# Gate weights loaded in the scan, five gate products in its last read-out, and the first output panel ahead of the residual stream

## The chip, the cores and the metric

The kernel runs on one core of a Trainium2 chip. One launch computes a two-part transformer block stack from its inputs. The metric is the device time of the launch in microseconds (us); lower is better.

## The reference, cut to what matters

The program runs two layers of a first block (attention mixed with an mLSTM, then an RWKV mixer, each followed by an MLP) and then a second block (gated linear attention, pooling, experts). The change touches the RWKV mixer's read-out and output of layer 1, on 512 tokens with 1024 channels (16 heads of 64):

```python
g = jax.nn.sigmoid(xg @ g1) @ g2          # g1: 1024 x 160, g2: 160 x 1024
...
def readout(p, y_f, y_b):
    y = y_f + y_b                         # the two scan directions
    mean = jnp.mean(y, axis=-1, keepdims=True)
    var = jnp.mean(jnp.square(y - mean), axis=-1, keepdims=True)
    y = ((y - mean) * lax.rsqrt(var + RW_GN_EPS)).reshape(r.shape) * lnx_w + lnx_b
    coef = ...                            # sum of r * k_dir * r_k over directions and head
    bonus = (coef * split_heads(v, RW_HEADS, RW_HEAD_DIM)).reshape(r.shape)
    return ((y + bonus) * g).astype(h_l.dtype) @ w_o
x = x + gt_a * out_l                      # then the MLP of the layer
```

## The kernel before, in words

Activations lie transposed: channels on the 128 partitions, tokens along the columns, so 1024 channels are eight blocks m = 0 to 7. A `Kernel` object K hands each engine its own in-order list of instructions; producers count up one semaphore per engine, and consumers wait for a count. `fence(name)` (line 54) makes an engine wait until every engine has reached the same place; TensorE's own count is part of it. PSUM has eight banks of 128 by 512, handed out in turn by `K.bank` (line 169), which waits until the bank's last reader is done.

Large products are written as three fp32r products (high by high, high by low, low by high) by the class `Split` (line 700): ScalarE copies half a weight panel to a rounded version (`act`, line 717, with the instruction on line 720), VectorE subtracts it from the original (`dve`, line 722, instruction on line 725), and TensorE then runs the products (line 750). Small products, the gate's among them, are plain fp32, and each of these stands in the trace as two MATMUL records.

The scan is `rw_pe`, `rw_act`, `rw_dve` and `rw_pool`, all driven by one list of steps, `rw_turns` (line 2421). There are 24 units (8 blocks m by 3 token ranges) for each of two directions d, and twelve turns per unit. In each turn stand the steps `solve` of unit n, `prep` of unit n + 1, `stream` of unit n - 1, and the steps `end` of the block before: six steps of the read-out of block m (0: the sum of the directions on VectorE; 1: the mean's product on TensorE, line 2584, and the centring on VectorE, line 2742; 2: ScalarE's square, line 2867; 3: the variance's product, line 2588, VectorE, line 2746, and logarithm and exponential on ScalarE; 4: the product for `coef`, line 2592, scaling on VectorE, copy on ScalarE; 5: two VectorE operations, the last on line 2758). For blocks 0 to 6 these steps lie beside the scan of the next block. For block 7 nothing else is left on any engine.

Then comes the fence "rwkv". Behind it the output stage runs:
- SyncE (`rw_out_sp`, line 2941) issues, in this order, the load of the residual stream from its spill in DRAM into `K.Xf` (2 MB), the two panels of `w_o` (2 MB each), and the MLP's first panel (2 MB). Later panels wait for a free slot.
- GpSimd (`rw_out_pool`, line 2947) loads `g2` in two pieces, 128 rows (512 KB) and 32 rows (128 KB).
- TensorE (`rw_out_pe`, line 2953) waits for both, then forms the eight gate blocks, each as a product over 128 rows (line 2958) and one over 32 rows (line 2959), and then the products with `w_o` in four groups g of two output blocks.
- VectorE (`rw_out_dve`, line 2981) does `w.dve(0)`, then for each block m multiplies the read-out by the gate (line 2988) and, one block behind, subtracts the rounded version (line 2992), then `w.dve(1)`, then per output block the residual addition (line 3001).
- ScalarE (`rw_out_act`, line 2966) does `w.act(0)` and `w.act(1)`, rounds the eight gated blocks (line 2972), and then goes on to the other panel halves and the squares for the next norm.

In the scan GpSimd (`rw_pool`, line 2879) first loads nine constants and four lora tiles; per unit it then multiplies gains (lines 2906, 2908), `kr` (2915), the operands `bb`, `ks` (2920, 2922) and `rr` (2925), and in `stream` scales the state (2933). `K.load` is on line 183, panels on line 192.

Of the kernel before, what the change touches and what calls it, by code (L numbers as in the profile page):

```python
# [542 lines left out]
def plan_layer1(K, w_at):  # L543
    a = K.a1 = Box()
    a.vec, a.wa0, a.gh = K.Cf[:, 1984:2024], K.alloc(32), K.alloc(2, 512)
    K.align()
    a.mix_lo, a.mixf = K.rounded(K.top, 8, 772), K.flat(8 * 772)
    a.mix = a.mixf.rearrange("p (k t) -> p k t", k=8)
    a.kT = a.mixf[:, 0:6144].rearrange("p (k t) -> p k t", k=8)
    r_at = K.top  # L550
    a.r_lo, a.rT = K.rounded(K.top, 8, 768), K.alloc(8, 768)
    hp_at, hpf = K.top, K.flat(8 * 772)
    mark = K.top - 32
    a.hp = hpf.rearrange("p (k t) -> p k t", k=8)
    a.vT = hpf[:, 0:6144].rearrange("p (k t) -> p k t", k=8)
    a.hi = K.rounded(K.top, 8, 768)
    K.alloc(8, 768)
    a.xx_lo, a.xx = K.rounded(K.top, 8, 772), K.alloc(8, 772)
    K.top = r_at
    a.w1, a.a1, a.g1 = K.alloc(8, 128), K.alloc(8, 128), K.alloc(8, 160)  # L560
    a.mu, a.wh, a.ah = K.Cf[:, 0:48], K.Cf[:, 64:832], K.Cf[:, 832:1600]
    K.top = hp_at
    a.g2 = K.alloc(2, 1024)
    K.align()
    a.rhi, a.wo = K.rounded(K.top, 8, 512), K.rounded(K.top + 4096, 4096)
    K.alloc(8192)
    K.top = mark
    r = K.rw = Box()
    bk1 = K.alloc(512)
    keep = K.top  # L570
    K.top = w_at
    r.cn = {n: K.const(n) for n in ("m16_0", "m16_1", "m32_0", "m32_1", "m64_0", "m64_1", "i64", "si_0", "si_1")}
    r.kk = [K.alloc(768) for _ in range(2)]
    bk = [K.row, bk1]
    r.dirs = []
    ybufs = []
    for d in range(2):
        s = Box()
        s.NP, s.M, s.Pf = K.alloc(2, 4, 64), K.alloc(4, 64), K.alloc(4, 64)
        far = K.Xf[:, 2048 * d:2048 * d + 1280]  # L580
        s.sets = [(K.alloc(2, 4, 64), K.alloc(4, 2, 64), K.alloc(4, 64), K.alloc(2, 4, 64)),
                  (far[:, 0:512].rearrange("p (x g c) -> p x g c", x=2, g=4),
                   far[:, 512:1024].rearrange("p (g x c) -> p g x c", g=4, x=2),
                   far[:, 1024:1280].rearrange("p (g c) -> p g c", g=4),
                   bk[d].rearrange("p (a g c) -> p a g c", a=2, g=4))]
        s.RH, s.UU = K.alloc(64), [K.alloc(64) for _ in range(2)]
        s.zm, s.zg = [K.alloc(64) for _ in range(2)], K.alloc(64)
        s.tmp = [K.alloc(256) for _ in range(5)]
        s.ops = [K.alloc(4, 256) for _ in range(3)]
        s.me = [K.alloc(3, 2) for _ in range(3)]  # L590
        s.gn = [K.alloc(2) for _ in range(3)]
        s.wm = [K.alloc(2, 128) for _ in range(2)]
        r.dirs.append(s)
        ybufs += [K.alloc(512) for _ in range(2)]
        if d == 0:
            K.top = keep
    r.sq, r.kavh = K.alloc(768), K.Cf[:, 2024:2032]
    r.V = [K.Xf[:, o:o + 768].rearrange("p (x c) -> p x c", c=64) for o in (1280, 3328)]
    r.y = K.ring("y", ybufs)
    r.kr = K.several("kr", 4, 512)  # L600


def plan_block2(K):
# [1765 lines left out]
UNITS, TURNS = 24, 12  # L2369
# [51 lines left out]
def rw_turns(K):  # L2421

    for n in range(-2, UNITS + 2):
        for turn in range(TURNS):
            if (n + 2) % 3 == 0 and (n + 2) // 3 < 8 and turn <= 5:
                yield "kk", turn, (n + 2) // 3
            for d in range(2):
                if 0 <= n < UNITS:
                    yield "solve", turn, Unit(K, d, n)
                if 0 <= n + 1 < UNITS and turn in PREP:  # L2430
                    yield "prep", PREP[turn], Unit(K, d, n + 1)
            for d in range(2):
                if 1 <= n <= UNITS:
                    yield "stream", turn, Unit(K, d, n - 1)
            m, since = divmod(n, 3)
            if since < 2 and 1 <= m and turn + TURNS * since in END:
                yield "end", END[turn + TURNS * since], m - 1


def halves():  # L2440
    for hd in range(2):
        yield hd, slice(64 * hd, 64 * hd + 64)


def rw_pe(K):
    a, pe = K.a1, K.pe
# [24 lines left out]
    for what, turn, u in rw_turns(K):  # L2471
# [65 lines left out]
        if what == "stream":  # L2537
# [22 lines left out]
            if part == 2:  # L2560
                pe.wait_ge(K.at("uu in", *c), K.at("BK", *u.key))
                done = [("streamed", *c)] + ([("streamed", *u.key)] if sub == 3 else [])
                if u.next(sub):
                    ps = K.bank("zz", *c)
                    for k, w in enumerate((uu, vm)):
                        for hd, o in halves():
                            mm = pe.e.matmul(ps[o, 0:64], u.BK[o, k, g, :], w[o, :], start=k == 0, stop=k == 1,  # L2567
                                             skip_group_check=True)
                    mm.then_inc(*pe.up(("zz", *c), *([] if u.lat else done)))
                if u.lat:  # L2570
                    ps = K.bank("y", *c)
                    pe.wait_ge(K.at("Arb", *u.key))
                    sums = (zm, u.rr[:, cs]), (uu, u.Arb[:, g, :]), (vm, u.A[:, g, 1, :])
                    for k, (w, A) in enumerate(sums):
                        for hd, o in halves():
                            mm = pe.e.matmul(ps[o, 0:64], w[o, :], A[o, :], start=k == 0, stop=k == 2, skip_group_check=True)  # L2576
                    mm.then_inc(*pe.up(("y", *c), *done))
        if what == "end":
            m, y0, k0 = u, K.rw.y.of(0, u), K.rw.kr.of(0, u)
            y1 = K.rw.y.of(1, u)  # L2580
# [298 lines left out]
def rw_pool(K):  # L2879
# [10 lines left out]
        K.load(pool, K.rw.cn[n], K.const_src(n), "rw const", n)  # L2890
    for d in range(2):
        weights(d, 0)
    for what, turn, u in rw_turns(K):
        if what == "prep":
            s = u.s
# [2 lines left out]
            if turn == 3:  # L2898
                if u.b == 2 and u.m < 7:
                    weights(u.d, u.m + 1)  # L2900
                pool.wait_ge(K.at("me exp", *u.key))
                if u.n >= 3:
                    pool.wait_ge(K.at("streamed", u.d, u.n - 3))
                if u.b:
                    last = Unit(K, u.d, u.n - 1)
                    pool.e.tensor_tensor(u.gn[:, 0:1], last.me[:, 2, last.xl[1]:last.xl[1] + 1],
                                         u.me[:, 0, u.xl[0]:u.xl[0] + 1], MUL).then_inc(*pool.up())
                pool.e.tensor_tensor(u.gn[:, 1:2], u.me[:, 2, u.xl[0]:u.xl[0] + 1], u.me[:, 0, u.xl[1]:u.xl[1] + 1],
                                     MUL).then_inc(*pool.up(("gain", *u.key)))
            if turn == 4 and u.lat:  # L2910
                if u.b == 1:
                    s.kb, free_k = K.rw.kr.take(u.d, u.m)
# [26 lines left out]


def rw_out_sp(K):
    K.load(K.sp, K.Xf, K.spill, "rw back")
    for i in range(2):
        K.panel_in(K.D["w_o"][i], "rw out", i)


def rw_out_pool(K):
    D, a, pool = K.D, K.a1, K.pool
    K.load(pool, a.g2[:, 0, :], D["g2"][0:128, :], "g2")
    K.load(pool, a.g2[0:32, 1, :], D["g2"][128:160, :], "g2 rest")  # L2950


def rw_out_pe(K):
    a, pe = K.a1, K.pe
    pe.wait_ge(K.at("g2"), K.at("g2 rest"))
    for m in range(8):
        ps = K.bank("rw gate", m)
        pe.e.matmul(ps, a.g2[:, 0, m * 128:m * 128 + 128], a.gh[:, 0, :], start=True, stop=False)
        pe.e.matmul(ps, a.g2[0:32, 1, m * 128:m * 128 + 128], a.gh[0:32, 1, :], start=False, stop=True).then_inc(
            *pe.up(("rw gate", m)))  # L2960
    for g in range(4):
        through(rw_out(K).columns(g, "rw out", 2 * g, lambda k, x0, x1: (a.rhi[:, k, x0:x1], a.r_lo[:, k, x0:x1]), LAT,
                                  lambda k: K.at("rw out lo", k), wide=g == 0))
# [1 line left out]

def rw_out_act(K):
    a, s, w, mlp = K.a1, K.act, rw_out(K), Mlp(K, 1)
    for g in range(2):
        w.act(g)
    for k in range(8):  # L2970
        s.wait_ge(K.at("rw gated", k))
        s.e.activation(a.rhi[:, k, :], a.rT[:, k, 0:512], ACT.Copy).then_inc(*s.up(("rw out hi", k)))
    for m in range(8):
        if m in (0, 2):
            w.act(2 + m // 2)
# [4 lines left out]

def rw_out_dve(K):
    a, v, w, mlp, LP = K.a1, K.dve, rw_out(K), Mlp(K, 1), K.mod[1][:, 0, :]
    w.dve(0)
    for m in range(9):
        if m < 8:
            r = a.rT[:, m, 0:512]
# [2 lines left out]
        if m:  # L2989
            r = a.rT[:, m - 1, 0:512]  # L2990
            v.wait_ge(K.at("rw out hi", m - 1))
            v.e.tensor_tensor(a.r_lo[:, m - 1, 0:512], r, a.rhi[:, m - 1, :], SUB).then_inc(*v.up(("rw out lo", m - 1)))
    w.dve(1)
    v.wait_ge(K.at("rw back"))
    for m in range(8):
# [1093 lines left out]
def pool_program(K):  # L4089
# [14 lines left out]
    pool.wait_ge(K.at("rw spill"))  # L4104
    rw_pool(K)
    pool.fence("rwkv")
    rw_out_pool(K)
    Mlp(K, 1).sums.pool()
    pool.fence("rw out")
    sums2(K).pool()  # L4110
# [74 lines left out]
```

## Time and profile before

| what | value |
|---|---|
| median of 3 runs | 3717.08 us (3716.05 to 3722.02) |
| the profiled execution's own time | 3724.84 us |
| its span, first to last instruction | 3723.0 us |
| TensorE matmul busy | 3426.0 us, 92% |
| VectorE, ScalarE, GpSimd busy | 44%, 32%, 11% |
| mean granted TensorE clock | 0.956 |

The span is cut by stage in the program's order: layer 0 first, the RWKV scan from about 1515 to 2290 us, its output stage from 2302 to 2395 us, then the MLP, the second block and the experts. A granted clock of 1.00 is 2.4 GHz and 0.50 is 1.2 GHz. Times in views are microseconds from the start of the span.

### The profile page before, as it was taken

The page shows a single profiled execution, that of the slowest core. Times are in us where ns is not written, and L with a number is a line of the kernel's source. Part 1 is how long each engine was busy: PE and PEld are TensorE (multiplying, and loading weights), DVE is VectorE, ACT ScalarE, POOL GpSimd, SP SyncE. Part 2 cuts the span into 40 slices and gives each one's busy share as a digit, 9 for nine tenths or more (in the row PEclk, how much of TensorE's full clock was granted, in tenths as well). Part 3 has the DMA queues.
Part 4 walks back from the last instruction along what each step waited for, and adds up shares of the span by engine and source line. Part 5 has one row for each costly group of instructions (what it writes and reads, how often), then busy time and mean ns, then how long its engine had stood idle before and what let it go on. Part 6 is the DMA issues. An engine that isn't in the chain of part 4 may idle for free.

```text
span 3723.0 us, 79537 instructions
## 1 busy us (share of the span) xinstructions
PE 3426.0 (92%) x35550; PEld 2659.8 (71%) x35550; DVE 1632.2 (44%) x3121; ACT 1179.5 (32%) x2462; POOL 394.4 (11%) x616
## 2 busy tenths in 40 slices
PE   7898998999999799799999997999999899799998
PEld 5767877788888388688888895588878677433332
DVE  3354455433333732466666663443443474312112
ACT  3342233312212332355555543222233332200001
POOL 0000122000000100232222221000010300000000
PEclk8999999999999899899999997899999899799999
DMA  4493162211111110000000002122211122689996
GB/s 177 149 352 111 51 241 108 79 58 68 68 61 54 65 46 23 10 5 5 5 5 4 5 5 99 46 91 102 102 66 46 47 104 76 264 353 412 414 428 293
DMA packets 35237, 437.42 MB, mean 117 GB/s; under 512 B 5024, under 2 KB 5632, under 8 KB 9168
## 3 DMA queue, kind: packets, MB, share of 16 engines
q1 hardware_dynamic: 29664, 413.44, 27.8%
q0 software_dynamic: 5232, 18.89, 1.6%
q8 instruction: 280, 4.59, 0.5%
q14 instruction: 61, 0.50, 0.0%
HBM read 425.49 MB, written 6.82 MB: 116 GB/s over the span
## 4 chain that ended last, share of the span: by engine, by line
PE 80%; DMA 7%; DVE 6%; ACT 5%; issue 1%; POOL 0%; SPq 0%; DVEq 0%; ACTq 0%; POOLq 0%
PE ps L750 23%; PE ps L2045 8%; PE ps L2047 8%; PE ps L2046 8%; PE ps L2461 7%; PE ps L3816 6%; DMA part<-in_wu 4%; PE ps L2454 3%; PE ps L1005 2%; PE ps L2468 2%; PE ps L2576 1%; ACT L71 1%; PE ps L2567 1%; DMA part<-in_wd 1%; PE ps L1322 1%
## 5 line engine op out<-in xcount | busy, mean ns | idle before, releaser
L750 PE MATMUL ps<-part 128*128 128x256 f32 (+1 forms) x4848 | 879.3, 343 | 40.9 <-DVE part L990 15.5
L750 PEld LDWEIGHTS ps<-part 128*128 128x128 f32 x4848 | 756.5, 193 | 160.6 <-issue 19.1
L2045 PE MATMUL ps<-part 128*128 128x512 f32 (+1 forms) x1536 | 549.6, 358 | 18.0 <-DVE part L2092 11.4
L2046 PE MATMUL ps<-part 128*128 128x512 f32 (+1 forms) x1536 | 548.8, 357 | 0.0
L2047 PE MATMUL ps<-part 128*128 128x512 f32 (+1 forms) x1536 | 548.6, 357 | 0.0
L3816 PE MATMUL ps<-part 128*64 128x512 f32 x1536 | 374.8, 606 | 27.4 <-DMA part<-in_wg 12.2
L2069 DVE TENSOR_TENSOR part<-part 128x1024 fp32r<-128x1024 f32 x128 | 158.3, 1237 | 497.7 <-ACT part L2058 497.7
L2461 PE MATMUL ps<-part 64*64 64x64 f32 x9984 | 344.7, 220 | 20.5 <-ACT part L2784 11.9
L2461 PEld LDWEIGHTS ps<-part 64*64 64x64 f32 x9984 | 319.1, 136 | 51.2 <-ACT part L2784 12.9
L2045 PEld LDWEIGHTS ps<-part 128*128 128x128 f32 x1536 | 289.7, 189 | 68.5 <-DVE part L2092 12.6
L2046 PEld LDWEIGHTS ps<-part 128*128 128x128 f32 x1536 | 290.5, 189 | 46.9
L2047 PEld LDWEIGHTS ps<-part 128*128 128x128 f32 x1536 | 289.7, 189 | 47.1
L3816 PEld LDWEIGHTS ps<-part 128*64 128x64 f32 x1536 | 119.6, 139 | 262.9 <-issue 201.9
L2058 ACT ACTIVATE part<-part 128x1024 fp32r<-128x1024 f32 x128 | 135.5, 1059 | 489.9 <-PE ps L2047 489.9
L725 DVE TENSOR_TENSOR part<-part 128x2048 fp32r<-128x2048 f32 x54 | 123.5, 2292 | 264.8 <-ACT part L720 264.6
L840 POOL TENSOR_TENSOR part<-part 128x512 f32<-128x512 f32 (+1 forms) x42 | 49.2, 1181 | 1217.2 <-ACT part L832 1216.7
L720 ACT ACTIVATE part<-part 128x2048 fp32r<-128x2048 f32 x58 | 110.4, 1910 | 95.0 <-PE ps L750 71.4
L3893 DVE TENSOR_TENSOR part<-part,ps 128x512 f32<-128x512 f32 x32 | 22.0, 687 | 244.6 <-PE ps L3790 115.1
L2454 PE MATMUL ps<-part 64*64 64x64 f32 (+1 forms) x2816 | 110.1, 229 | 11.3 <-DVE part L2661 11.3
L2454 PEld LDWEIGHTS ps<-part 64*64 64x64 f32 x2816 | 101.6, 137 | 11.7 <-DVE part L2661 11.7
L2833 ACT ACTIVATE part<-ps 128x512 f32<-128x512 f32 x144 | 75.2, 529 | 92.3 <-PE ps L2461 92.3
L2468 PE MATMUL ps<-part 64*64 64x64 f32 x2688 | 95.9, 219 | 0.8 <-DVE part L2697 0.6
(418 smaller groups left out, 4362.9 us busy)
## 6 DMA issues: line engine op xcount, KB each, us to landing
part<-in_ada_w SPq DMA_DIRECT2D x36, 2048.0 KB, 9.7
part<-in_mlp_w SPq DMA_DIRECT2D x32, 2048.0 KB, 7.5
part<-in_wg SPq DMA_DIRECT2D x32, 2048.0 KB, 14.1
part<-in_wu SPq DMA_DIRECT2D x32, 2048.0 KB, 13.0
part<-in_wd SPq DMA_DIRECT2D x32, 2048.0 KB, 14.3
part<-in_b_in SPq DMA_DIRECT2D x8, 2048.0 KB, 7.7
part<-in_ab_w_in SPq DMA_DIRECT2D x7, 2048.0 KB, 8.3
part<-in_rkv SPq DMA_DIRECT2D x6, 2048.0 KB, 7.5
```

The lines of the kernel that those rows point to most:

```text
L720: s.e.activation(self.first(g), self.tile(g), ACT.Copy).then_inc(*s.up((name, "rounded", g), (name, "split", g)))
L725: v.e.tensor_tensor(self.rest(g), self.tile(g), self.first(g), SUB).then_inc(*v.up((name, "split", g)))
L750: mm = pe.e.matmul(ps[:, j * n:j * n + n], lhs, rhs, start=k == ks[0] and i == 0, stop=k == ks[-1] and i == 2)
L2045: pe.e.matmul(ps, wh[:, k, :], hi[:, k, x0:x1], start=k == 0, stop=False)
L2046: pe.e.matmul(ps, wh[:, k, :], lo[:, k, x0:x1], start=False, stop=False)
L2047: mm = pe.e.matmul(ps, wl[:, k, :], hi[:, k, x0:x1], start=False, stop=k == 7)
L2058: s.e.activation(b.W[t % 2][0], src, ACT.Copy).then_inc(*s.up(self.key("rounded", t), self.key("split", t), *([("free", "w") + self.key("w ...
L2069: v.e.tensor_tensor(wl, src, wh, SUB).then_inc(*v.up(self.key("split", t), *([("free", "w") + self.key("w", p)] if c == 3 else [])))
L2454: mm = pe.e.matmul(out[o, 2 * it + j], lhs[o, t], rhs[o, :, t], start=True, stop=True)
L2461: mm = pe.e.matmul(ps[h, o + g * 64:o + g * 64 + 64], lhs[h, g, :], rhs[h, g, :], start=True, stop=True)
L2468: mm = pe.e.matmul(ps[h, o + i * 64:o + i * 64 + 64], block[h, :], K.ident[h, h], start=True, stop=True)
L3816: mm = pe.e.matmul(ps[half(p), :], lhs(k, p), K.panel(8, 512, w, g, c, p)[:, k, :], start=k == 0, stop=k == 7)
```

## The change

The second piece of `g2` gets two places of its own that are free during the scan (`rest`, and one at the end), and the first piece takes the place in `K.Cf` where the lora inputs of the scan lay. GpSimd issues the two loads of the second piece at the head of the scan, and the load of the first in the preparation of the last unit, once the last lora products have read that place. Gate blocks 0, 1 and 2 to 4 are issued by TensorE within the read-out of block 7, after its steps 0, 2 and 4; blocks 5 to 7 stay behind the fence. SyncE loads the first panel of `w_o` ahead of the residual stream and the second panel behind it. ScalarE rounds gated blocks 0 to 5, then does `w.act(0)`, then blocks 6 and 7, then `w.act(1)`; VectorE does `w.dve(0)` after all the gated blocks. The arithmetic is unchanged.

```diff
@@ plan_layer1
     K.top = hp_at
-    a.g2 = K.alloc(2, 1024)
+    K.alloc(2048)
...
         if d == 0:
+            rest = K.alloc(512)
             K.top = keep
...
+    a.g2, a.g2r = K.Cf[:, 64:1088], [rest, K.alloc(512)]
@@ rw_turns
             if since < 2 and 1 <= m and turn + TURNS * since in END:
                 yield "end", END[turn + TURNS * since], m - 1
+                if m == 8 and END[turn + TURNS * since] in (0, 2, 4):
+                    yield "gate", END[turn + TURNS * since], None
...
+def gate_pe(K, m):
+
+    a, pe = K.a1, K.pe
+    ps = K.bank("rw gate", m)
+    c = slice(m % 4 * 128, m % 4 * 128 + 128)
+    pe.wait_ge(K.at("g2"), K.at("g2 rest", m // 4))
+    pe.e.matmul(ps, a.g2[:, m * 128:m * 128 + 128], a.gh[:, 0, :], start=True, stop=False)
+    pe.e.matmul(ps, a.g2r[m // 4][0:32, c], a.gh[0:32, 1, :], start=False, stop=True).then_inc(*pe.up(("rw gate", m)))
@@ rw_pe
+        if what == "gate":
+            for m in {0: (0,), 2: (1,), 4: (2, 3, 4)}[turn]:
+                gate_pe(K, m)
         if what == "end":
@@ rw_pool
     for d in range(2):
         weights(d, 0)
+    for i in range(2):
+        K.load(pool, a.g2r[i][0:32, :], D["g2"][128:160, i * 512:i * 512 + 512], "g2 rest", i)
...
+            if turn == 4 and u.n == UNITS - 1 and u.d:
+                pool.wait_ge(*[K.at("lora", d, UNITS - 1) for d in range(2)])
+                K.load(pool, a.g2, D["g2"][0:128, :], "g2")
             if turn == 4 and u.lat:
@@ rw_out_sp
-    K.load(K.sp, K.Xf, K.spill, "rw back")
     for i in range(2):
         K.panel_in(K.D["w_o"][i], "rw out", i)
-
-
-def rw_out_pool(K):
-    D, a, pool = K.D, K.a1, K.pool
-    K.load(pool, a.g2[:, 0, :], D["g2"][0:128, :], "g2")
-    K.load(pool, a.g2[0:32, 1, :], D["g2"][128:160, :], "g2 rest")
+        if i == 0:
+            K.load(K.sp, K.Xf, K.spill, "rw back")
@@ rw_out_pe
-    pe.wait_ge(K.at("g2"), K.at("g2 rest"))
-    for m in range(8):
-        ps = K.bank("rw gate", m)
-        pe.e.matmul(ps, a.g2[:, 0, m * 128:m * 128 + 128], a.gh[:, 0, :], start=True, stop=False)
-        pe.e.matmul(ps, a.g2[0:32, 1, m * 128:m * 128 + 128], a.gh[0:32, 1, :], start=False, stop=True).then_inc(
-            *pe.up(("rw gate", m)))
+    for m in range(5, 8):
+        gate_pe(K, m)
@@ rw_out_act
-    for g in range(2):
-        w.act(g)
     for k in range(8):
         s.wait_ge(K.at("rw gated", k))
         s.e.activation(a.rhi[:, k, :], a.rT[:, k, 0:512], ACT.Copy).then_inc(*s.up(("rw out hi", k)))
+        if k == 5:
+            w.act(0)
+    w.act(1)
@@ rw_out_dve
-    w.dve(0)
     for m in range(9):
...
+    w.dve(0)
     w.dve(1)
     v.wait_ge(K.at("rw back"))
@@ pool_program
-    rw_out_pool(K)
```

## Rows read from the trace of the kernel before

**Rows 1.** The page: shares of the chain that ended last.

```profile
PE 80%; DMA 7%; DVE 6%; ACT 5%; issue 1%; POOL 0%; SPq 0%; DVEq 0%; ACTq 0%; POOLq 0%
```

**Rows 2.** The chain of waits, 2288 to 2395 us: start, length, who held it.

```profile
2288.73 0.94 PE ps L2576 x24
...
2290.76 1.14 PE ps L2584 x2
2291.92 0.70 DVE part L2742
2292.65 0.64 ACT part L2867
2293.33 2.09 PE ps L2588 x2
...
2300.98 0.70 DVE part L2758
...
2302.90 13.42 DMA part<-in_g
2316.45 2.04 PE ps L2958 x2
...
2348.54 46.29 PE ps L750 x192
```

**Rows 3.** Windows: length, busy time of the five engines, granted clock, DMA share, GB/s.

```profile
2284.00:2290.00 6.00, 5.35 (x144) 4.55 (x140) 1.13 (x4) 3.14 (x14) 0.59 (x2) 1.00 0.02 5
2290.00:2293.00 3.00, 1.12 (x2) 0.30 (x2) 2.47 (x4) 0.35 (x1) 0.00 (x0) 0.92 0.00 0
2293.00:2295.00 2.00, 1.67 (x2) 0.84 (x3) 0.00 (x0) 0.28 (x1) 0.00 (x0) 0.50 0.00 0
...
2328.40:2336.40 8.00, 8.00 (x9) 2.00 (x8) 2.58 (x4) 1.26 (x2) 0.00 (x0) 0.50 0.00 0
...
2352.00:2360.00 8.00, 8.00 (x33) 6.50 (x32) 0.85 (x1) 0.00 (x0) 0.00 (x0) 0.88 0.00 0
```

**Rows 4.** Timeline and window of the lora products of line 2299, about 1290 us.

```profile
1283.86 14.29 PE L2299 MATMUL ps<-part 128*128 128x512 f32 x28
...
1282.80:1298.00 15.20, 15.20 (x31) 3.18 (x30) 15.13 (x19) 4.88 (x11) 0.00 (x0) 1.00 0.00 1
```

**Rows 5.** Timeline of GpSimd, and its DMAs of line 183 from 1480 us on.

```profile
1528.93 0.35 POOL L2908 TENSOR_TENSOR part<-part 128x1 f32<-128x1 f32 x1 [13.51 <-ACT part L2805]
...
2234.17 0.73 POOL L2915 TENSOR_TENSOR part<-part 128x256 f32<-128x256 f32 x1 [2.26 <-DVE part L2654]
2235.26 0.73 POOL L2915 TENSOR_TENSOR part<-part 128x256 f32<-128x256 f32 x1 [0.36 <-DVE part L2654]
...
2240.19 1.59 POOL L2925 TENSOR_TENSOR part<-part 128x256 f32<-128x256 f32 x2 [0.96 <-ACT part L2811]
...
L183 POOL DMA_DIRECT2D part<-in_w x16: 524/536/577, 1513.3 to 2143.0; - x16
...
DMA to landing us min/median/max: 1.9/2.1/13.4
```

**Rows 6.** DMA issues of 2270 to 2420 us; then line 192's (five panels) landing.

```profile
part<-spill SPq DMA_DIRECT2D x1, 2048.0 KB, 8.5
...
DMA to landing us min/median/max: 7.4/14.7/23.5
```

**Rows 7.** Timeline of the output stage: single operations of VectorE and ScalarE.

```profile
2319.00 2.29 DVE L725 TENSOR_TENSOR part<-part 128x2048 fp32r<-128x2048 f32 x1 [17.33 <-ACT part L720]
...
2324.54 0.69 DVE L2988 TENSOR_TENSOR part<-part,ps 128x512 f32<-128x512 f32 x1 [2.65 <-PE ps L2959]
2325.14 0.68 DVE L2992 TENSOR_TENSOR part<-part 128x512 fp32r<-128x512 f32 x1
2325.26 0.63 ACT L2972 ACTIVATE part<-part 128x512 fp32r<-128x512 f32 x1 [2.70 <-DVE part L2988]
...
2362.27 1.92 ACT L720 ACTIVATE part<-part 128x2048 fp32r<-128x2048 f32 x1 [12.35 <-PE ps L750]
```

## The prediction

> **What bounds the kernel now.** I read the page first: TensorE is 92% busy and holds 80% of the chain that ended last [rows 1], so only what leaves that chain counts. The change touches one place, from the end of the recurrent scan to the first product with `w_o`, so the next view is the chain of waits over that stretch. It shows four pieces in a row [rows 2]. The last scan product ends at 2288.73 + 0.94 = 2289.67 us. The read-out of the last column block goes back and forth between the engines until VectorE's last addition ends at 2300.98 + 0.70 = 2301.68, which opens the fence. Then a DMA of the gate's weights holds everything until 2316.3. Then sixteen gate products, two for each of eight blocks, run to 2348.54, where the first product with `w_o` starts. From the fence to that product it is 2348.54 - 2301.68 = 46.9 us, of which 14.8 us are the wait and 32.1 us the gate.
>
> The third view is the windows of that stretch. One fp32 product of 512 columns takes 32.1 / 16 = 2.00 us here [rows 2], and the granted clock is 0.50 (1.2 GHz) in all of it, although TensorE is 100% busy [rows 3]. The clock was 1.00 (2.4 GHz) in the scan, 0.92 over 2290 to 2293, and 0.50 from 2293 on, after TensorE had worked 1.12 of 3 us. It came back only under the `w_o` products. At 1.00 the same kind of product costs half: before the r, k, v projections a run of alternating products, 128 by 128 and 128 by 32, of 512 columns kept 1.00 throughout and did 28 records (14 products) in 14.29 us, so 1.02 us each [rows 4]. One block of the gate is thus 4.01 us at half clock and 2.04 us at full.
>
> **Part 1: the weights are loaded in the scan.** This removes the wait of 14.6 us for the DMA. It adds three DMAs on GpSimd. The two of the 32 remaining rows stand at the head of the scan behind 13 others of the same kind; at about 0.53 us of issue each [rows 5] they end before GpSimd's first arithmetic there; I take 0, at worst 2 x 0.53 = 1.1 us. The large one stands in unit 23's preparation, d = 1. Its wait for the lora products is one that the engine's next input already implies. It costs 0.53 us of issue between the two `kr` products of 2234.17 and 2235.26. Between these GpSimd was idle 0.36 us, and the 0.2 us left over meets an idle 0.96 us ahead of `rr` [rows 5]. Behind the load wait the products that make unit 23's operands, and TensorE's gram behind these. I take 0, at most 0.5 us. It has from about 2235 to 2289.7 to land; 13.4 us was the slowest of GpSimd's DMAs, under 8 MB of other traffic [rows 6].
>
> **Part 2: five gate blocks in the last read-out.** TensorE takes its work in program order, so each product that is put ahead can delay the read-out. At full clock, from 2289.67:
> - gate 0 runs to 2291.7. The mean's product was ready at 2290.76 [rows 2], so it is 0.95 us late and ends at 2292.8 (two records, about 1.0 us).
> - gate 1 runs to 2294.8. VectorE's centring, 0.70, and ScalarE's square, 0.64, would have released the variance's product at 2294.3 [rows 2], so it starts 0.5 us late and ends at 2295.9; `coef` at 2296.9; gates 2, 3 and 4 (6.1 us) at 2303.0.
> - the rest of the read-out took 2301.68 - 2295.42 = 6.26 us from the end of the variance's product [rows 2]; now it ends at 2302.1.
>
> The fence counts TensorE's work too, so it opens at 2303.0, 1.3 us later than before. The five blocks and the three others with the read-out take exactly the eight PSUM banks; all were freed before.
>
> Whether these products hold the full clock is the disputed cost, since no row has a product of 32 rows at 1.00. Bounds: 2.04 us a block by [rows 4], 4.01 by [rows 2]. I take 2.04, because TensorE goes without a gap from the scan into them, and a run with every second product narrow kept its clock [rows 4]; the runs at 0.50 all began after idling. Against this stands that 32 us of such work did not bring the clock back [rows 3].
>
> The Trainium skill (TensorE: Matmul & The Clock Gate, section "Why this matters for your kernels") says that continuous matmul work takes the array to its full clock and that idle gaps between bursts take it back. The trace agrees with the second half and not with the first: the gate ran 32 us without a gap at 0.50. By the rule the five blocks run at full clock, as I take it, and the three behind the fence do so as well.
>
> **Part 3: behind the fence (F = 2303.0).** Gate 5 needs the bank that VectorE frees with its first product, at F + 0.8. At full clock gates 5, 6, 7 end at F + 2.8, 4.9, 6.9. VectorE multiplies (0.69), ScalarE rounds (0.63), VectorE subtracts (0.68) [rows 7]; overlapped, a block costs VectorE about 1.26 us, so block 5 is multiplied by F + 6.6 and rounded by F + 7.3. Now ScalarE does `w.act(0)` (1.92), which needs the first panel. Before, that panel was second in SyncE's queue and landed 14.7 us after its issue; the first in the queue, the residual stream, took 8.5 us, and a panel alone 7.4 [rows 6]. I take 8.1, so the rounding runs from F + 8.2 to F + 10.1. Then block 6 is rounded by 10.8 and subtracted by 11.5, block 7 by 12.1, and `w.dve(0)` (2.29) ends at 14.4. The first `w_o` product starts at F + 14.5 = 2317.5. Cover: gate 7's end (F + 6.9) has 1.5 us of slack before VectorE's turn for it at F + 8.4; at half clock it would end at F + 12.8. The start then is late by the chain behind the gate: 0.69 + 0.63 + 0.69 + 2.29, so at F + 17.2.
>
> **Part 4: panel order.** The residual stream now lands second, within 15 us, and is wanted first more than 10 us after the first `w_o` product. Panel 1 is third in the queue as before. Both cost 0. The second half's split is done before it is needed: 1.92 on ScalarE and 2.29 on VectorE lie beside about 11.6 us of the first products.
>
> **Sum.** 2348.54 - 2317.5 = 31.0 us less: 14.6 of wait, 32.1 of gate and 0.2 of issue leave; 1.3 comes before the fence and 14.5 behind it. The `w_o` products begin at half clock before and after, since TensorE idles ahead of them in both; I allow 1 us either way for when it rises. What follows is paced by TensorE, and SyncE's panels are released by its products, so it moves with it. The profiled execution takes 3724.84 - 31.0 = 3693.8 (span 3692), and it was 7.8 us above the median. The median: 3717.08 - 31.0 = 3686.
>
> **The rivals.**
> - A, the clock falls as before, after the mean's product. Gate 1 at half clock ends at 2296.8, variance 2298.8, `coef` 2300.8, three gates 2312.9. F is 2312.9, the start F + 17.2 = 2330.1: 18.4 us gained, 3698.7. For it: [rows 3], where the 32-row products never raised the clock, and the fall near 2292.5. Against it: the fall came after a stretch mostly idle, and now there is none. 14%.
> - B, the first panel comes no sooner than it did, after 14.7 us, because transfers queued behind it share the engines. ScalarE then splits from F + 14.9 to 16.8, and block 6, block 7 and the rest follow 6.7 us late: start F + 21.2 = 2324.2, 24.3 us gained, 3692.8. For it: 14.7 in [rows 6]. Against it: the queue's first took 8.5. 10%.
> - C, slower: the gate's large load lands late. Gate 0 then blocks TensorE's queue in front of the mean's product, and its price is the landing less 2289.7. The change turns slower at landings past 2320.7, 86 us after GpSimd's turn; one at 2330 costs 9 net: 3726. Against it: small loads land in 2.0 us and the longest took 13.4 [rows 5, 6]. 2%.
> - D, no change: the fence opens later by what leaves behind it, because the read-out is paced by the gate. It would take 31 us more ahead of the fence, and all five blocks at half clock are 20 us. 1%.
>
> **How the numbers follow.** My forecast has 73%, with its own range 3682 to 3691 (panel landing between 7.4 and 8.6, clock rise 1 us, issue costs to 1.6 us, drift between measurements 2 us). The range for 8 in 10 runs from 3681 to 3699 and takes in B and most of A. A measurement of this kernel can tell 0.2%, 7.4 us, from no change: every case but C and D is below 3709.6, so faster 0.97, same 0.01, slower 0.02.
>
> **What would show it.** Right: granted clock near 1.00 up to the fence, with gate records near 0.6 us; the mean's product starting at scan end + 2.0; no idle time for a load of `g2`; the fence 13.3 us after the scan's end (12.0 before); the first `w_o` product 14.5 us behind it, the last thing before it being VectorE's subtraction of the panel. Wrong: 0.50 within the read-out (A), ScalarE waiting beyond F + 9 for `w_o` (B), TensorE waiting for `g2` at the scan's end (C), or a scan longer by over 1 us.

## The result, and the profile after

| | before | after |
|---|---|---|
| median, first comparison | 3717.84 us (3716.05 to 3722.02, 4 runs) | 3690.47 us (3686.91 to 3693.23, 4 runs) |
| ratio, 95% interval | | 0.9919 (0.9907 to 0.9931) |
| median, repeat | 3719.7 us (9 runs) | 3690.4 us (3687.49 to 3695.69, 5 runs), ratio 0.9919 (0.9905 to 0.9933) |
| profiled execution: own time, span | 3724.84, 3723.0 us | 3686.91, 3685.1 us |
| scan's end to the first `w_o` product | 58.9 us | 26.8 us |
| scan's end to the MLP's first product | 113.1 us | 80.8 us |

The ratio makes the changed kernel 30.1 us faster (25.7 to 34.6); the medians differ by 27.4 and 29.3 us. The forecast was 31.0. The changed kernel is faster clear of the noise. The profiled execution of before was its slowest and that of after its fastest, so their spans differ by 37.9 us: 1.7 us of that lie ahead of the scan's end, where both run the same code but for the three loads of `g2`, 32.4 us in the stretch that was changed, and 3.8 us behind it.

The chain of waits of the changed kernel over the read-out and the output stage (start, length, who held it) answers to [rows 2]; lines 2456 and 2457 are the two products of a gate block:

```profile
2287.01 0.92 PE ps L2591 x24
2287.92 1.05 PE ps L2456 x2
2288.98 1.05 PE ps L2457 x2
2290.03 1.06 PE ps L2602 x2
...
2292.99 1.06 PE ps L2606 x2
...
2299.98 1.06 PE ps L2457 x2
2301.04 0.02 issue
2301.06 7.55 DMA part<-in_w_o
2308.61 0.02 issue
2308.64 1.91 ACT part L723
2310.55 0.53 ACT part L2984
2311.07 0.02 issue
2311.10 1.29 DVE part L3006 x2
2312.39 2.21 DVE part L728
2314.60 0.14 issue
2314.74 5.41 PE ps L753 x13
```

The chain is now TensorE without a gap from the scan's end, 2287.92, to the fence at 2301.04, then the first panel's landing, then the splits. The gate's load has gone from it. The windows show the clock; their columns are those of [rows 3]:

```profile
2291.00:2295.00 4.00, 4.00 (x10) 1.47 (x9) 1.38 (x2) 0.83 (x2) 0.00 (x0) 1.00 0.00 0
2295.00:2301.00 6.00, 6.00 (x12) 1.48 (x10) 2.62 (x4) 2.94 (x4) 0.00 (x0) 1.00 0.00 0
2301.00:2308.50 7.50, 6.39 (x13) 1.77 (x12) 7.25 (x12) 3.67 (x6) 0.00 (x0) 1.00 0.89 339
2308.50:2314.70 6.20, 0.00 (x0) 0.00 (x0) 4.93 (x7) 4.75 (x4) 0.00 (x0) 0.56 1.00 428
2314.70:2318.00 3.30, 3.26 (x8) 2.62 (x9) 2.10 (x1) 0.00 (x0) 0.00 (x0) 0.50 1.01 432
```

Where the read-out had 0.50 before, it has 1.00, and so have the three blocks behind the fence here. TensorE then idles 6.5 us and begins `w_o` at half clock, as before. On GpSimd the large load stands where it was expected, in the timeline that answers to [rows 5]:

```profile
2231.25 0.73 POOL L2938 TENSOR_TENSOR part<-part 128x256 f32<-128x256 f32 x1 [2.26 <-DVE part L2672]
2231.92 0.60 POOL L183 DMA_DIRECT2D part<-in_g  x1
2232.54 0.74 POOL L2938 TENSOR_TENSOR part<-part 128x256 f32<-128x256 f32 x1
```

### The profile page after: what moved, and what is told of

It is laid out like the page before. It is cut to its first block, busy times and chain, and to the rows that moved or that the text cites. A ratio compares the mean times of both kernels' runs of the same rounds, so it can differ in the third digit from the quotient of the medians.

```text
span 3685.1 us, 79537 instructions
## 1 busy us (share of the span) xinstructions
PE 3399.3 (92%) x35550; PEld 2654.1 (72%) x35550; DVE 1632.4 (44%) x3121; ACT 1178.6 (32%) x2462; POOL 394.9 (11%) x617
## 4 chain that ended last, share of the span: by engine, by line
PE 80%; DMA 7%; DVE 6%; ACT 5%; issue 1%; POOL 0%; SPq 0%; DVEq 0%; ACTq 0%; POOLq 0%
PE ps L753 23%; PE ps L2048 8%; PE ps L2050 8%; PE ps L2049 8%; PE ps L2476 7%; PE ps L3831 6%; DMA part<-in_wu 4%; PE ps L2469 3%; PE ps L2483 2%; PE ps L1008 1%; PE ps L2591 1%; ACT L71 1%; PE ps L2582 1%; PE ps L1325 1%; PE ps L3711 1%
## 5 line engine op out<-in xcount | busy, mean ns | idle before, releaser
L2469 PEld LDWEIGHTS ps<-part 64*64 64x64 f32 x2816 | 102.2, 137 | 12.1 <-DVE part L2679 12.1
```

The costliest lines, as they stand in the source:

```text
L2469: mm = pe.e.matmul(out[o, 2 * it + j], lhs[o, t], rhs[o, :, t], start=True, stop=True)
```

## The experiments

A place in the stage is given in us from the end of the last scan product: +16.3 is 16.3 us behind it. Each such figure is of one profiled execution. Edits are against the changed kernel.

### All eight gate blocks behind the fence

```diff
@@ rw_turns
-                if m == 8 and END[turn + TURNS * since] in (0, 2, 4):
-                    yield "gate", END[turn + TURNS * since], None
@@ rw_out_pe
-    for m in range(5, 8):
+    for m in range(8):
@@ gate_pe
-    pe.e.matmul(ps, a.g2r[m // 4][0:32, c], ...
+    pe.e.matmul(ps, a.g2r[1][0:32, c], ...
```

> The changed kernel with all eight gate blocks behind the fence and none in the read-out; the loads stay in the scan, the panel order and the order on ScalarE and VectorE stay (blocks 0 to 3 use the narrow weights of blocks 4 to 7, so the values differ, not the work). Measured from the end of the last scan product to the first w_o product, which is 58.9 us before and 26.8 us after. Theory: TensorE idles in the read-out, the granted clock falls to 0.50, and blocks with a 32-row product do not bring it back: fence at +12.0, eight blocks at 4.01 us, then 0.69 + 0.63 + 0.69 + 2.29, so 48.7 us; gain over before 10 us, near 3708. Rival: continuous matmul work brings the clock back in some 5 us as it did under the w_o products: block at 2.1 us after that, 36 us in all, near 3695.

Measured: 3712.54 us (10 runs), ratio 0.9977 (0.9968 to 0.9986); first `w_o` product 47.8 us from the scan's end. The windows:

```profile
2296.00:2300.00 4.00, 3.72 (x4) 1.00 (x4) 0.06 (x1) 0.00 (x0) 0.00 (x0) 0.50 0.74 233
2300.00:2312.00 12.00, 12.00 (x13) 3.00 (x12) 3.27 (x5) 1.89 (x3) 0.00 (x0) 0.50 1.01 431
2312.00:2328.40 16.40, 16.37 (x17) 4.00 (x16) 5.16 (x8) 4.32 (x5) 0.00 (x0) 0.50 0.32 139
```

TensorE is busy for 32 us at half clock: near the theory's 48.7, and not the rival's 36. So the early loads with the new order behind the fence are worth 11.1 of the 32.1 us, and the five blocks in the read-out the other 21.0. How these divide between the clock and the place, the next run tells.

### The narrow products made full height, for the clock alone

```diff
@@ gate_pe, on top of the edit before
-    pe.e.matmul(ps, a.g2r[1][0:32, c], a.gh[0:32, 1, :], start=False, ...
+    pe.e.matmul(ps, a.g2[:, m * 128:m * 128 + 128], a.gh[:, 0, :], start=False, ...
```

> As the run with all eight blocks behind the fence, but the second product of each block takes 128 rows (the first product's operands once more) in place of 32; the gate's values are wrong, the number and the columns of the products are the same. Theory (the 32-row products are what kept the clock down): the clock rises within some 5 us of the first block and the rest run at 2.1 us, 36 us from the scan's end to the first w_o product. Rival (fp32 products of any height do not bring the clock back from idle): 0.50 throughout and 48.7 us.

Measured: 3695.28 us (one run); first `w_o` product at 32.1 us. The timeline of TensorE from its first gate product:

```profile
2302.43 2.05 PE L2454 MATMUL ps<-part 128*128 128x512 f32 x2 [5.62 <-issue]
2304.26 1.92 PE L2455 MATMUL ps<-part 128*128 128x512 f32 x2
2305.97 1.63 PE L2454 MATMUL ps<-part 128*128 128x512 f32 x2
2307.44 1.02 PE L2455 MATMUL ps<-part 128*128 128x512 f32 x2
2308.30 1.02 PE L2454 MATMUL ps<-part 128*128 128x512 f32 x2
```

Sixteen products of the same columns, all 128 rows high, bring the clock back after 4.8 us. So the alternation with 32 rows is what held it down in [rows 3], and not fp32, nor the idle time alone; one execution shows it. The rival is refuted. With all eight blocks still behind the fence, `w_o` starts 15.7 us earlier than in the run before and 5.3 us later than in the changed kernel: of the 21.0 us, three quarters come without moving a block, most of them by the clock and 2 to 3 us by the closer spacing told next (an estimate, 0.39 us on each of some seven blocks). Only a quarter is left for the place of the five blocks.

A second thing shows: the products follow each other at 0.86 us, a block in 1.72, where the alternating heights take 1.05 and 2.11. The theory's 36 was 4 us too high, most of it because it had 2.1 for a block. The height is not what adds the 0.2 us, though. The products of [rows 4] are all 128 rows high and alternate in width, 128 and 32 (the view of line 2299, 1283.5 to 1290.5 us, kernel before), and they take 1.02 us each:

```profile
L2299 PE MATMUL ps<-part x15: 592/592/697, 1283.3 to 1290.5; 128*128 128x512 f32 x8, 128*32 128x512 f32 x7
```

So the edit took away two things, the 32 rows and the change of shape, and the rise of the clock is not shown to hang on the rows alone. The change of shape did not make the clock fall in [rows 4]; no run starts such products at half clock. Nor does every product under 128 rows keep the clock down: in the scan of the kernel before, TensorE had stood idle 11.3 us until 1534.40, then ran products of 64 by 64, and the clock rose to 1.00 at 1538.1 (length, TensorE's busy time, granted clock, DMA share and GB/s):

```profile
1534.70:1538.10 3.40, 3.40 (x66) 0.50 0.02 5
1538.10:1542.00 3.90, 3.72 (x93) 0.99 0.00 2
```

### Gate blocks 0 to 4 after the read-out's last product

```diff
@@ rw_pe
-            for m in {0: (0,), 2: (1,), 4: (2, 3, 4)}[turn]:
+            for m in {0: (), 2: (), 4: (0, 1, 2, 3, 4)}[turn]:
```

> The changed kernel with blocks 0 to 4 all issued after the product for coef, none between scan and mean or mean and variance. Same instructions, same fence. Theory: the gaps of the read-out take the clock down as before, and the five blocks then run at 4.01 us: coef ends at +7.5, the blocks at +27.5, fence there, three more blocks at half clock, first w_o product 17.2 us later, 44.7 us in all; near 3704. Rival: only the number of products counts and they run at full clock: fence at +18.0, first w_o product at 31.8 us, near 3691.

Measured: 3693.17 us (4 runs), ratio 0.9920 (0.9899 to 0.9940); first `w_o` product at 31.4 us. My theory fell here:

```profile
2291.10:2295.20 4.10, 1.54 (x3) 1.00 0.01 4
2295.20:2298.70 3.50, 3.50 (x5) 0.51 0.00 0
2298.70:2306.00 7.30, 7.30 (x15) 1.00 0.00 0
2306.00:2315.20 9.20, 9.14 (x18) 1.00 0.60 223
```

(Columns as in the two lines above.) The gaps did take the clock, but it came back 3.4 us later, under the variance's product, `coef` and the 128-row product of gate 0, which stand back to back. From 1.00 the blocks keep it. The rival's 31.8 is nearly what was measured, 31.4, for another reason than it gave. Blocks 0 and 1 in their early places, with the fall of the clock that they avoid, gain 4.6 us in the stage; the total cannot tell that.

### The residual stream first again

```diff
@@ rw_out_sp
-        K.panel_in(K.D["w_o"][i], "rw out", i)
         if i == 0:
             K.load(K.sp, K.Xf, K.spill, "rw back")
+        K.panel_in(K.D["w_o"][i], "rw out", i)
```

> The changed kernel with the residual stream again ahead of the first w_o panel in SyncE's queue. Theory: the panel lands 13 to 14.7 us after its issue in place of 7.6, ScalarE's rounding waits for it, and the first w_o product is 5.5 to 7.1 us later than in the changed kernel (32 to 34 us from the scan's end); near 3696. Rival (the transfer is hidden by VectorE's work on the gate): no later than 1 us.

Measured: 3699.07 us (3692.64 to 3701.9, 4 runs), ratio 0.9940 (0.9922 to 0.9957); first `w_o` product at 31.9 us, 5.1 us later. ScalarE's wait for the panel, in the view of waits (who, for whom, total, times, longest):

```profile
ACT part L723 <- DMA part<-in_w_o: 5.7, 1, 5.7
```

The wait was 0.5 us in the changed kernel. The panel landed 12.3 us after its issue, a little under the theory's 13, and the transfer is not hidden. The order of the two loads is worth 5.1 us against the profiled execution of the changed kernel, and 3.6 against that of its repeat below, whose clock fell at the same place as here. The intervals of the ratios overlap.

### The changed kernel once more

> The changed kernel once more, unchanged, on the same chip as the three runs beside it. Its first profiled execution was its fastest and that of the kernel before its slowest; the stage alone gained 32.1 us there. Theory: the stage's gain is fixed and the rest is scatter of the other stages: 26.8 us from the scan's end to the first w_o product again, and 27 to 34 us less than before in the whole time, near 3690. Rival (part of the gain is given back in later stages): under 27 us.

Measured: 3690.4 us, ratio 0.9919 (0.9905 to 0.9933), a difference of 30.1 us again; no sign that gain is given back. But the stage took 28.3 us to the first `w_o` product, not the 26.8 expected:

```profile
2294.50:2307.60 13.10, 13.09 (x26) 1.00 0.00 1
2307.60:2310.80 3.20, 2.34 (x5) 1.00 0.72 225
2310.80:2318.40 7.60, 7.55 (x8) 0.50 1.00 429
```

The clock fell at about +16.3, within the blocks behind the fence, and block 7 ended at +23.9 in place of +20.3, later than the panel. It fell there in four of six profiled executions with narrow blocks behind the fence (this, the residual-first run and both below with extra products), and at +21.3 or +21.4, after the blocks, in two (the first execution and the halves below). It costs 1.5 us here, for the panel's landing hides most of it.

The two kinds are told apart before the changed code is reached. In the four, the last stretch at 0.50 within the scan ends 45 us ahead of its end; in the two, 43.5 us ahead of it, and it is twice as long. The repeat, then the first execution (columns as above):

```profile
2246.00:2249.40 3.40, 3.28 (x22) 0.50 0.01 2
2237.60:2244.30 6.70, 6.03 (x70) 0.50 0.01 4
```

So where the clock falls behind the fence goes with this and not with the edits of the runs with narrow blocks, and each must be held against the execution of its own kind: first `w_o` product at 28.3 and the MLP's at 82.5 for those that fall at +16.3, 26.8 and 80.8 for the others.

### The first group in halves

```diff
@@ rw_out_act
         if k == 5:
-            w.act(0)
+            rw_half_act(K, 0)          # k blocks 0 to 3 of group 0
+            rw_half_act(K, 1)          # k blocks 4 to 7
@@ rw_out_dve: the subtraction of gated blocks 6 and 7 moves behind
+                rw_half_dve(K, 0)
+                rw_half_dve(K, 1)
@@ rw_out_pe
-                                  lambda k: K.at("rw out lo", k), wide=g == 0))
+                                  lambda k: K.at("rw out half", 1) if g == 0 and k in (4, 5) else K.at("rw out lo", k), wide=g == 0))
```

> The changed kernel with the first w_o group split in two halves of four k blocks on ScalarE and VectorE, both halves rounded ahead of gated blocks 6 and 7, and the subtraction of the halves ahead of that of gated blocks 6 and 7. Theory: the chain behind the panel's landing (7.55 us after its issue) shrinks from 6.1 us to 0.97 + 1.15 and some waits, so the first w_o product starts 23.1 us after the scan's end, 3.7 us earlier; if the granted clock then outlives the 2.9 us of idle time, another 2.3 us. Total 3.7 to 6 us below the changed kernel. Rival (something else is late behind it: gated blocks 6 and 7 when the products reach k = 6): the w_o products stall and the gain is under 1 us.

Measured: 3685.4 us (5 runs), ratio 0.9908 (0.9895 to 0.9921); first `w_o` product at 23.2 us, 3.6 us earlier than in the first execution, which is of its kind, and as expected. The intervals of the ratios overlap. The clock did not outlive the 2.9 us pause, and the products did not stall at k = 6.

### The halves, and two unread products

```diff
@@ rw_out_pe
     for m in range(5, 8):
         gate_pe(K, m)
+    ps = K.bank("warm")
+    for i in range(2):
+        mm = pe.e.matmul(ps, a.g2[:, 0:128], a.gh[:, 0, :], start=True, stop=True)
+    mm.then_inc(*pe.up(("free", "ps", "warm")))
```

> The run with the halves, and behind the last gate block two more products of gate block 0's shape (128 rows, 512 columns, fp32) into a spare bank that nobody reads, 1.7 us of TensorE. Theory (an idle stretch is what takes the clock): the clock stays at 1.00 into the w_o products, the 192 of them take 41.5 to 42 us in place of 46.0, and the total is 6 us below the changed kernel. Rival (the clock falls anyhow, or did not fall with the halves alone): same as with the halves alone, within 0.5 us in the stage.

Measured: 3685.98 us (4 runs), ratio 0.9905 (0.9892 to 0.9919). A miss in the stage: the clock fell at +16.2 already, as in the repeat, ahead of the extra products, which then ran at half speed too, and the first `w_o` product came at 26.7 us. So whether two extra products can keep the clock that reaches them is not tested here.

### Six unread products alone

The edit is the one above with `range(6)`, without the halves.

> The changed kernel with six such unread products behind the last gate block (5.2 us), the rest as in the changed kernel. Theory: the w_o products start at the same 26.8 us, but at clock 1.00, and the 192 take about 2.3 us less than 46.0. Rival (the w_o products' first microseconds are slow for another reason, the SBUF traffic of the DMAs at 432 GB/s): no difference in the 46.0 us.

Measured: 3686.65 us (one run). The clock fell at +16.3 here as well, so the first `w_o` product came at 30.0 us, not 26.8:

```profile
2301.90:2312.20 10.30, 10.30 (x11) 0.51 1.01 431
2312.20:2316.00 3.80, 3.80 (x11) 0.99 1.04 444
2316.00:2330.00 14.00, 14.00 (x62) 1.00 0.28 118
```

The 128-row products brought the clock back, beside transfers of 444 GB/s, and the 192 `w_o` products took 44.1 in place of 46.2 us. So their slow start is the clock and not the transfers. Against the repeat, whose clock fell at the same place, they start 1.7 us later and take 2.0 less: the MLP's first product comes at 82.1 in place of 82.5, so it comes out about even.

### Full height with the values kept

```diff
@@ rw_pool, head of the scan
     for i in range(2):
+        pool.e.memset(a.g2r[i], 0.0).then_inc(*pool.up(("g2 empty",)))
+    pool.wait_ge(pool.now())
+    for i in range(2):
@@ rw_in_dve
+    v.e.memset(a.gh[:, 1, :], 0.0).then_inc(*v.up(("gh empty",)))
@@ gate_pe
-    pe.e.matmul(ps, a.g2r[m // 4][0:32, c], a.gh[0:32, 1, :], start=False, ...
+    pe.e.matmul(ps, a.g2r[m // 4][:, c], a.gh[:, 1, :], start=False, ...
```

> The changed kernel with the narrow product of each gate block made 128 rows high: the tiles of its weights are set to zero once at the head of the scan (two memsets on GpSimd) and the upper rows of gh once in layer 1's input stage (one on VectorE), and the values stay the same. Theory (rows of height 32 are what lets the clock fall within the blocks, and the change of height is what leaves 0.2 us of each weight load open): a block takes 1.7 us in place of 2.1, the granted clock stays 1.00 through all eight, the fence opens at +12.9 in place of +13.1 us from the scan's end, and the first w_o product starts at +26.6, never at the 28.3 of the repeat. Total 0 to 1.5 us below the changed kernel. Rival (the clock falls after the fence for the 0.9 us pause, whatever the rows): last blocks at half clock again in some executions, +28.

Measured: 3687.44 us (5 runs), ratio 0.9909 (0.9894 to 0.9924). The last block ended at +17.9 in place of +20.3, and the first `w_o` product came at 25.3 us, 1.3 earlier than expected: the fence opened sooner, since VectorE's last addition ends at +11.6. The eight blocks ran at 1.00, and the clock fell at +21.3, in the idle time behind them. But this execution is of the kind in which the narrow blocks kept the clock too, so it does not decide between theory and rival. The total is 3 us below the changed kernel, inside the noise.

### All three together

The edits are those of the full height, of the halves and of the unread products, four of them.

> All three steps together: full-height blocks, the first w_o group in halves ahead of gated blocks 6 and 7, and four unread products (128 rows, 3.4 us) behind the last block. Theory: first w_o product at +23.1 us from the scan's end, at clock 1.00, the 192 products in 41.5 to 42 us in place of 46.0; the next stage starts 7.5 to 8 us earlier than in the changed kernel; total near 3682. Rival (the clock falls at a place set by something else): 192 products in 45 to 46 us, total near 3686.

Measured: 3683.91 us (3675.38 to 3691.04, 6 runs), ratio 0.9898 (0.9879 to 0.9916). Windows of TensorE from the scan's end on:

```profile
2289.10:2300.80 11.70, 11.38 (x28) 1.00 0.01 1
2300.80:2310.80 10.00, 8.82 (x20) 1.00 0.92 364
2310.80:2330.00 19.20, 19.13 (x84) 1.00 0.58 249
```

The clock never fell in this stage, with a pause of 1.2 us at the fence, although this execution is of the kind that lost it at +16.3 with narrow blocks, four times out of four. That speaks against the rival. First `w_o` product at 21.8 us, the 192 products in 43.8 us, the MLP's first product at 73.5 us where the changed kernel has 80.8. The median is 6.5 us below the repeat of the changed kernel, near the 7.2 of the stage, but the intervals of the two ratios overlap: only the profiles show it. The 41.5 to 42 us expected for the 192 products were too low: at 1.00 from the first one and without a gap they take 43.8, so the full clock is worth 2.2 to 2.4 us there. This run has the lowest median of the study.

## Why the prediction was right

- The wait for the gate's weights went, as Part 1 had it, and the issue of the large load (0.60, forecast 0.53) met idle time.
- Part 2 held: the fence came 13.1 us after the scan's end, forecast 13.3. The disputed term, 2.04 us for a block at full clock, measured 2.11, against the other end of 4.01. The clock stayed at 1.00 over all five blocks in all six executions that had narrow blocks so placed. The reason that I gave, no gap between the scan and the blocks, is half of it: gaps took the clock in the run with the late blocks too, and 128-row products back to back brought it to 1.00 again. Blocks with a 32-row product each did not bring it back in 32 us, which the first two experiments show side by side.
- Part 3 was 0.8 us too long: the panel landed after 7.55 us, forecast 8.1, and the chain behind it took 6.1, forecast 6.4. With these the first `w_o` product came at 26.8, forecast 27.8, so the stage gained 32.1 where the sum said 31.0.
- The slack of 1.5 us that I gave gate 7 at full clock was there, but I did not expect its clock to fall on the way: in four of six executions it did, for 1.5 us in the repeat. That the first execution, with its 26.8, was one of the other two is luck; at 28.3 the gain of the stage is 30.5, near the forecast all the same. This is rival A at another place, behind the fence, where most of it is hidden.
- Part 4 held: the residual stream landed 12.1 us after its issue and nobody waited for it. Rival B was wrong in this order and right in the other: put behind the residual stream, the panel came 5.1 us later from the fence on.
- Rivals C and D did not show. The gate's load was there in time in every run.

The forecast of 3686 for the median was 4.5 us low. By the ratio the gain is 30.1 us, so 0.9 of that is the forecast and the rest the scatter of the medians, the one I started from included.

## What to carry to other kernels

Small products behind a fence can cost far more than their durations suggest: the eight gate blocks took 32 us there at half clock, 4.0 each, and 2.1 us each at full clock once they stood close behind busy TensorE work. The clock is the largest part of this gain, so look for it before the place. Put each such product where the next step of the tail is not ready yet, and count what it adds to the fence. Where a short contraction is left over, fill it up with zeros to the full height if that is cheap: here a block then takes 1.72 us in place of 2.11, and in the one execution that could tell it kept the clock.

## What the runs showed of the hardware that was not expected

- Granted clock and shape: 32 us of unbroken work, half of it products of 32 rows, stayed at 0.50 (in the kernel before and in the run with all blocks behind the fence); the same count of 128-row products rose to 1.00 after 4.8 us (one execution). Products of 64 by 64 alone brought it back too, within 3.7 us. Whether the 32 rows or the change of shape from product to product keeps it down stays open.
- Started at 1.00, the mixed blocks held it for 13 us in six executions, and in four of them lost it at +16.3, after a pause of 0.9 us at the fence. With full-height blocks and a pause of 1.2 us it was kept in an execution of that kind. One execution shows it, so the pause's own part stays open. The loss at +16.3 went with a last stretch at half clock in the scan that ended 45 us ahead of the scan's end, and not 43.5 us.
- fp32 products of 512 columns follow each other at 0.86 us at full clock when their shape stays 128 by 128, and at 1.02 to 1.05 us when it changes from one to the next, in height (the gate) or in width ([rows 4]).
- The executions differ before the changed code is reached: the scan ended between 2285.0 and 2296.8 us over the eleven profiled executions of the changed kernel and its variants, although nearly all of the code ahead of it is the same. This scatter, and not the stage, sets how finely the totals can be told apart.
